# A diffusion-style block chain on one core: first modulation vectors by TensorE, and new places for the tiles

## The chip, the cores and the metric

The program runs on 1 core of a Trainium2 chip. The metric is the device time of one execution in microseconds. Everything is fp32 in memory; the big products use fp32r operands.

## What is computed

Two blocks in a row work on a sequence x of 512 tokens by 1024 features; the second also carries a context of 256 tokens. What matters here is how each norm is modulated: a condition vector c of 1024 numbers, through a SiLU, times a matrix w_ada, gives shift, scale and gate vectors of 1024 numbers each.

```python
def first_block(x, c, w_ada, b_ada, ...):
    c_act = jax.nn.silu(c)
    mod = c_act @ w_ada[l] + b_ada[l]                 # 6 vectors of 1024
    sh1, sc1, g1, sh2, sc2, g2 = jnp.split(mod, 6, axis=-1)
    h = _rmsnorm(x, norm_attn_g[l]) * (1.0 + sc1) + sh1
    proj = h @ w_in[l]                                # 3600 columns
    y = concat(dilated_attention(...), gated_deltanet(...)) @ w_out[l]
    x = x + g1 * y
    h = _rmsnorm(x, norm_ffn_g[l]) * (1.0 + sc2) + sh2
    x = x + g2 * ((silu(h @ w_gate[l]) * (h @ w_up[l])) @ w_down[l])
    return _rmsnorm(x, final_norm_g)

def second_block(x, c, ctx, c_ctx, ...):              # 2 layers
    # per layer: 9 vectors for the sequence and 9 for the context;
    # half step of a feed-forward, mixers (Fourier, attention, gating, pooling), half step
```

## The kernel before

**Products.** A big product x @ w is made by TensorE in three passes over fp32r halves: high(w) with high(x), high(w) with low(x), low(w) with high(x) (L2099, L2100, L2101 in this order; L2112 to L2114 where two blocks of weights go through the tiles in turn). A block of weights is 128 by 1024 numbers (8 tiles of 128 by 128); SyncE's queue loads it into one of 4 stage buffers (L1652), ScalarE rounds it to its high half (L1771), VectorE subtracts for the low half (L2544). The operand that streams is a tile of x with the 512 tokens of the sequence, or the 256 of the context, as columns: `hn_high`/`hn_low` after a norm, `hidden_high`/`hidden_low` inside a feed-forward, `mixed_high`/`mixed_low` after the mixers.

**Modulation.** `modulation` (16 calls in the opening, the others as background between the products) takes a block of w_ada as 128 partitions by 8 steps by 128 columns. The partitions are four quarters of 32, each for other columns; a partition holds 32 rows of the matrix in four parts; four DMAs, one for each quarter of the partitions, load a block. VectorE multiplies it by the condition and adds, 8 instructions per block (L2626 the first, L2629 the rest), and after four blocks TensorE sums over the partitions with two fp32 products (L2164), whose result gets the bias (L2634).

**Opening.** `first_block` starts with 16 such blocks: the vectors for scale and shift of the first norm. Between them it turns the tokens (L2205, four 128 by 128 transposes for each of 8 feature tiles), squares them (L1830) and sums the squares with fp32 products of one column (L2174), takes the root, and makes the rows of distances for the attention's bias (L2214, then a DMA out and back). `gains`, `modulated_norm` and the first products with w_in follow. Each engine walks the same program and runs its own part of it in order, with semaphores between the engines; a wait keeps everything behind it on its engine.

**Places.** `Memory` gives out the bytes of a partition in order. The permanent tiles come first (hidden state, stage, halves of the weights, the square buffers); the maps of the phases (`start_maps`, `first_maps`, `ffn_maps`, `mixer_maps`) then lie over each other from `phase_base` on. Before the change phase_base lies at 192 modulo 512:

```python
ROW, LANE = 512, 192
self.at += (LANE - self.at) % ROW     # before phase_base
self.at += (LANE - self.at) % 128     # before hn_first of the first block
```

As every tile in those maps is a multiple of 512 bytes long, except the padded convolution input (12 x 515 numbers), the streaming operands start at these places modulo 512: 448 for the first block's norm, 192 for its mixed tiles, for all tiles of the feed-forwards and for norm and mixed tiles of the mixers. The weights' halves start at 128.

Of the kernel before, what the change touches and what calls it, by code (L numbers as in the profile page):

```python
# [18 lines left out]
ALU = mybir.AluOpType  # L19
# [3 lines left out]
P = 128  # L23
# [22 lines left out]
QROWS = D // 32  # L46
ROW, LANE = 512, 192
COMPUTE = ("tensor_wrote", "scalar_wrote", "vector_wrote", "pool_wrote")
# [109 lines left out]
class Memory:  # L158


    def __init__(self, nc, ctx, inp, const, out):
# [22 lines left out]
        self.small_consts = sb("small_consts", [P, P])  # L184
        self.at += (LANE - self.at) % ROW
        self.phase_base = self.at
# [12 lines left out]
    def place(self, name, shape, dtype=F32):  # L199
        size = 4 * int(np.prod(shape[1:]))  # L200
        assert self.at + size <= SBUF_END, (name, self.at + size - SBUF_END)
        self.names += 1
        t = self.nc.alloc_sbuf_tensor_at(f"{name}_{self.names}", shape, dtype, offset=self.at)
        self.at += (size + 31) // 32 * 32
        return t

    def area(self, name, n):
# [8 lines left out]
    def start_maps(self):  # L216
# [30 lines left out]
        self.tokens_main = self.area("tokens", 4 * D).rearrange("p (a n) -> p a n", a=4)  # L247
        self.cond_rows = self.area("cond_rows", 3 * QROWS).rearrange("p (c n) -> p c n", c=3)
        self.table = self.area("table", SKEW)[0:N_BUCKETS + 1]
        self.relb = self.area("rel_bias", HEADS1)[0:N_BUCKETS + 1]  # L250
# [6 lines left out]
    def first_maps(self):  # L257
# [4 lines left out]
        self.G, self.EG, self.BT = (self.area("gate_rows", SEQ)[0:8] for _ in range(3))  # L262
        self.at += (LANE - self.at) % 128
        delta_base = self.at
# [20 lines left out]
        self.pick_pair = self.spread[0:8, 0:4, :]  # L285
        self.at = after_norms
        self.Y = self.halves("mixed", KT, SEQ)
        self.YD = self.tiled("delta_out", 4, SEQ)
# [4 lines left out]
    def ffn_maps(self):  # L293
        self.at = self.phase_base
        self.ffn_hn, self.hidden = {}, {}
        for name, T in (("ctx", CTX), ("main", SEQ)):
            self.ffn_hn[name] = self.halves("hn", KT, T)
            self.hidden[name] = self.halves("hidden", GROUPS[0][1], T)

    def mixer_maps(self):  # L300
# [5 lines left out]
        self.mixer = {"main": main, "ctx": side}  # L306
        for m, T in ((main, SEQ), (side, CTX)):
            m.T, m.nt, hn_at = T, T // P, self.at
            m.hn = self.halves("hn", KT, T)
            after, self.at = self.at, hn_at  # L310
            m.YS = self.halves("mixed", KT, T)
            m.YT = []
            for half in range(2):
                self.at = hn_at + 4 * (half * KT + 2) * T
                m.YT += [self.area("head_fourier", 2 * GW) for _ in range(T // GW)]
            self.at = after
# [81 lines left out]
class Walk:  # L398
# [82 lines left out]
    def load(self, n):  # L481
        w, k0, nk, c0, cols, split = self.board.plan[n]
        stage = self.stages.next()
        raw = stage.ap[:, 0:nk * cols]
        dst, at, moves = raw.rearrange("p (k n) -> p k n", k=nk), 0, []
        if isinstance(k0, tuple):
            rows = w.rearrange("(p r) n -> p r n", r=QROWS)[:, k0[0]:k0[0] + nk]
            moves = [(dst[32 * q:32 * q + 32], rows[:, :, c0 + q * P:c0 + (q + 1) * P]) for q in range(4)]
        for c, width in () if moves else (c0 if isinstance(c0, tuple) else ((c0, cols),)):
            moves.append((dst[:, :, at:at + width], w[k0:k0 + nk * P, c:c + width].rearrange("(k p) n -> p k n", p=P)))  # L490
            at += width
        self.load_block(n, stage, moves)
        return stage, raw
# [294 lines left out]
    def distance_bias(self):  # L788
        self.distance_tables()
        for o, n in ((0, 512), (512, SKEW - 512)):  # L790
# [816 lines left out]
    modulation_vector = clear = load_start = turn_vectors = condition = turn_tokens = distance_tables = idle  # L1607
    load_first = load_conditions = distance_rows = store_distances = skew_distances = token_square = token_pair = token_pair_sums = turn_context = gate_logs = gate_sums = gate_exps = turn_gates = load_bias = attention_scores = attention_turn = attention_values = idle
    attention_normalise = head_square = head_roots = head_spread = gains = clear_pads = gate_row = idle
# [9 lines left out]
class Sync(Walk):  # L1619


    def load_first(self):
        self.dma(self.misc(), ("eye",), self.mem.eye[:], self.mem.const["eye"])
        self.wait_ge("cleared")
        for n, (tile, dst, src) in enumerate(self.mem.rows):
# [3 lines left out]
    def load_start(self):  # L1629
        mem, i = self.mem, self.mem.inp  # L1630
        col = lambda ap: ap.rearrange("(n o) -> n o", o=1)
        self.dma(self.misc(), ("tokens", "main"), mem.tokens_main, i["x"][0].rearrange("(a p) n -> p a n", p=P))
        self.dma(self.misc(), ("small", 0), mem.dt_bias, col(i["dt_bias"][0]))
# [131 lines left out]
class Scalar(Walk):  # L1765
# [44 lines left out]
    def load_conditions(self):  # L1810
        i = self.mem.inp
        for n, c in enumerate((i["c"][0], i["c_2"][0], i["c_ctx_2"])):
            sem, rows = "cond_landed" if n == 0 else "conds_landed", c.rearrange("(p r) -> p r", r=QROWS)
# [3 lines left out]
            self.board.new["cond_rows", n] = sem, self.dma_counts[sem]  # L1817

    def condition(self, n, x, t):
        self.wait_ge("cond_rows", 2 if n else 0)  # L1820
        self.wait_free(t)
# [261 lines left out]
class Tensor(Walk):  # L2083
# [65 lines left out]
    def root_of_both(self, main, twin, names, banks):  # L2149
# [389 lines left out]
class Vector(Walk):  # L2539
# [64 lines left out]
    def scale_tile(self, name, part, k, rinv, ready):  # L2604
# [3 lines left out]
            .then_inc(*self.mark("scaled", name, k))  # L2608

    def modulation_sums(self, name, n, view, part, vectors, quarter):  # L2610

# [433 lines left out]
```

## Time and profile before

| what | us |
|---|---|
| median of 3 runs | 3629.4 (3621.26 to 3639.6) |
| profiled execution | 3635.35 |
| its span, first to last instruction | 3633.3 |

The profile is one execution. PE stands for TensorE's matmuls, PEld for its weight loads, DVE for VectorE, ACT for ScalarE, POOL for GpSimd, SP for SyncE; SPq and ACTq are DMA issues on these queues. A program's fp32 product stands in the records as two instructions (two loads, two matmuls); an fp32r product and a transpose as one. A matmul's listed duration runs past the start of the next one, so prices are read from start to start.

### The profile page before, as it was taken

Reading aid. Unit: us, or ns where it says so; the run is one execution under the profiler, and the core shown is the slowest. Engines: PE = TensorE matmul, PEld = TensorE weight load, DVE = VectorE, ACT = ScalarE, POOL = GpSimd, SP = SyncE. Lnnn points to the kernel's source line nnn. Section 1 sums busy time; section 2 is a strip of 40 time slices with the busy share of each in tenths; the row PEclk is TensorE's granted clock in tenths of the full one; section 3 lists DMA queues with packets and bytes.
Section 4 is the critical chain, followed back from the end, with each engine's and each line's share of the span. In section 5 each row is a group of like instructions: output and inputs, shape, how many; then the busy total and the mean of one; then the engine's idle time right before and its main releaser. Section 6 shows DMA issues by size and latency. Waiting matters only on the chain. (4 is left out here: it accounts for less than half of the span.)

```text
span 3633.3 us, 49233 instructions
## 1 busy us (share of the span) xinstructions
PE 3441.9 (95%) x19911; PEld 2821.2 (78%) x19911; DVE 2148.4 (59%) x4936; ACT 1031.6 (28%) x1604; POOL 131.9 (4%) x116
## 2 busy tenths in 40 slices
PE   5988899999999999899999999989999999999998
PEld 4655867887888888774688888878888886578887
DVE  6554656567667575764455667676766636543334
ACT  3354023222321212243432121222122124432222
POOL 0012010000000000100000000010000010000000
PEclk9998979999999999898999999989999999999999
DMA  8532024444234343330023434333343413023331
GB/s 176 148 96 64 4 74 125 118 132 115 85 91 116 99 115 94 99 85 18 24 62 99 113 93 111 101 106 87 107 107 102 109 49 111 12 76 95 97 99 64
DMA packets 646938, 333.94 MB, mean 92 GB/s; under 512 B 31659, under 2 KB 642935, under 8 KB 646456
## 3 DMA queue, kind: packets, MB, share of 16 engines
q1 hardware_dynamic: 645812, 330.63, 33.4%
q8 instruction: 156, 2.56, 0.3%
q14 instruction: 70, 0.57, 0.1%
q10 hardware_dynamic: 900, 0.18, 0.0%
HBM read 328.61 MB, written 2.77 MB: 91 GB/s over the span
## 5 line engine op out<-in xcount | busy, mean ns | idle before, releaser
L2099 PE MATMUL psum<-hn_high,high 128*128 128x512 f32 (+1 forms) x3136 | 1116.1, 356 | 9.7 <-DVE low L2544 9.7
L2101 PE MATMUL psum<-hn_high,low 128*128 128x512 f32 (+1 forms) x3136 | 1110.5, 354 | 0.0
L2100 PE MATMUL psum<-hn_low,high 128*128 128x512 f32 (+1 forms) x3136 | 1107.5, 353 | 0.0
L2629 DVE SCALAR_TENSOR_TENSOR partial<-stage,cond,partial 128x128 f32<-128x128 f32 x2592 | 701.9, 346 | 0.0
L2099 PEld LDWEIGHTS psum<-hn_high,high 128*128 128x128 f32 x3136 | 591.6, 189 | 120.5 <-issue 21.0
L2100 PEld LDWEIGHTS psum<-hn_low,high 128*128 128x128 f32 x3136 | 591.7, 189 | 86.5 <-issue 0.5
L2101 PEld LDWEIGHTS psum<-hn_high,low 128*128 128x128 f32 x3136 | 591.1, 188 | 82.8
L2544 DVE TENSOR_TENSOR low<-stage,high 128x1024 fp32r<-128x1024 f32 (+2 forms) x415 | 493.1, 1208 | 187.8 <-ACT high L1771 187.3
L1771 ACT ACTIVATE high<-stage 128x1024 fp32r<-128x1024 f32 (+2 forms) x415 | 415.2, 1025 | 504.0 <-DMA stage<-in_w_ffn 354.8
L2099 PE MATMUL psum<-hidden_high,high 128*128 128x512 f32 (+1 forms) x1408 | 495.8, 352 | 2.0 <-DVE hidden_low L2549 2.0
L2101 PE MATMUL psum<-hidden_high,low 128*128 128x512 f32 (+1 forms) x1408 | 496.4, 353 | 0.0
L2100 PE MATMUL psum<-hidden_low,high 128*128 128x512 f32 (+1 forms) x1408 | 495.4, 352 | 0.0
L2872 DVE TENSOR_TENSOR tmp<-tmp,psum 128x512 f32<-128x512 f32 (+1 forms) x176 | 103.5, 588 | 389.6 <-PE psum L2101 389.2
L1775 ACT ACTIVATE hidden_high<-tmp 128x512 fp32r<-128x512 f32 (+1 forms) x176 | 97.1, 552 | 791.8 <-DVE tmp L2872 791.8
L2099 PEld LDWEIGHTS psum<-hidden_high,high 128*128 128x128 f32 x1408 | 267.6, 190 | 40.6 <-DVE hidden_low L2549 2.4
L2100 PEld LDWEIGHTS psum<-hidden_low,high 128*128 128x128 f32 x1408 | 267.5, 190 | 38.3
L2101 PEld LDWEIGHTS psum<-hidden_high,low 128*128 128x128 f32 x1408 | 267.4, 190 | 35.3
L1992 ACT ACTIVATE tmp<-psum 128x512 f32<-128x512 f32 (+1 forms) x176 | 91.2, 518 | 359.7 <-PE psum L2101 346.2
L2869 DVE TENSOR_TENSOR tmp<-tmp,psum 128x512 f32<-128x512 f32 (+1 forms) x176 | 102.7, 584 | 112.0 <-ACT tmp L1992 112.0
L2549 DVE TENSOR_TENSOR hidden_low<-tmp,hidden_high 128x512 fp32r<-128x512 f32 (+1 forms) x176 | 104.3, 593 | 108.8 <-ACT hidden_high L1775 108.8
L1731 POOL TENSOR_TENSOR mean_main<-mean_main,tmp 128x512 f32<-128x512 f32 x42 | 54.5, 1297 | 2726.5 <-ACT tmp L1793 2726.5
L2763 DVE SCALAR_TENSOR_TENSOR h_main<-psum,small,h_main 128x512 f32<-128x512 f32 x96 | 71.6, 746 | 75.2 <-PE psum L2101 75.0
(316 smaller groups left out, 2948.3 us busy)
## 6 DMA issues: line engine op xcount, KB each, us to landing
stage<-in_w_ffn SPq DMA_DIRECT2D x240, 512.0 KB, 4.2
stage<-in_w_ada SPq DMA_DIRECT2D x768, 128.0 KB, 2.8
stage<-in_w_in SPq DMA_DIRECT2D x48, 512.0 KB, 4.5
stage<-in_w_out SPq DMA_DIRECT2D x24, 512.0 KB, 4.1
stage<-in_w_ffn SPq DMA_DIRECT2D x32, 384.0 KB, 3.8
stage<-in_w_gate SPq DMA_DIRECT2D x22, 512.0 KB, 3.9
stage<-in_w_up SPq DMA_DIRECT2D x22, 512.0 KB, 5.1
stage<-in_w_down SPq DMA_DIRECT2D x16, 512.0 KB, 4.0
```

The source lines that it names most:

```text
L1771: self.e.activation(high, raw, ACT.Copy).then_inc(*self.mark("high", n))
L1775: self.e.activation(high, x, ACT.Copy).then_inc(*self.mark("high_half", key))
L1992: self.e.activation(s, ps_a, ACT.Sigmoid).then_inc(*self.mark("gate_sigmoid", key))
L2099: self.e.matmul(out, high[:, i], xh, start=first and n == 0, stop=False)
L2100: self.e.matmul(out, high[:, i], xl, start=False, stop=False)
L2101: done = self.e.matmul(out, low[:, i], xh, start=False, stop=last and n == nk - 1)
L2544: self.e.tensor_tensor(low, raw, high.bitcast(F32), ALU.subtract).then_inc(*self.mark("split", n))
L2549: self.e.tensor_tensor(low, x, high.bitcast(F32), ALU.subtract).then_inc(*self.mark(*key))
L2629: self.e.scalar_tensor_tensor(acc, view[:, k, :], by, acc, ALU.mult, ALU.add).then_inc(*inc)
L2763: self.e.scalar_tensor_tensor(h, ps, gate, h, ALU.mult, ALU.add).then_inc(*self.mark("residual", name, part.name, f))
L2869: self.e.tensor_tensor(s, s, ps_a, ALU.mult).then_inc(*self.mark("gated", key))
L2872: self.e.tensor_tensor(s, s, ps_b, ALU.mult).then_inc(*self.mark("gated_up", key))
```

## The change

The opening's 16 blocks are taken by TensorE: block j holds rows p*8 + k of w_ada (p the partition, k = j modulo 8) with 1024 columns, of the scale for j under 8 and of the shift after; it is loaded by one DMA in rows of 4 KB, and 8 fp32 products with the column k of the condition add to 8 columns of one PSUM bank. One VectorE instruction then adds the bias to all 16 columns. The condition of the first block gets a load and a SiLU of its own; the other conditions, the late vectors, the distance table and the tokens are loaded or taken at other points. The streaming operands of the sequence start at 384 modulo 512 and those of the context at 64.

```diff
-ROW, LANE = 512, 192
+ROW, MAIN_LANE, CTX_LANE = 512, 384, 64
...
-        self.at += (LANE - self.at) % ROW
+        self.lane(CTX_LANE)
         self.phase_base = self.at
...
+    def lane(self, at):
+        self.at += (at - self.at) % ROW
...
         self.G, self.EG, self.BT = (self.area("gate_rows", SEQ)[0:8] for _ in range(3))
-        self.at += (LANE - self.at) % 128
+        self.lane(MAIN_LANE)
         delta_base = self.at
...
         self.at = after_norms
+        self.lane(MAIN_LANE)
         self.Y = self.halves("mixed", KT, SEQ)
...
-        for name, T in (("ctx", CTX), ("main", SEQ)):
+        for name, T, lane in (("ctx", CTX, CTX_LANE), ("main", SEQ, MAIN_LANE)):
+            self.lane(lane)
...
-        for m, T in ((main, SEQ), (side, CTX)):
+        for m, T, lane in ((main, SEQ, MAIN_LANE), (side, CTX, CTX_LANE)):
+            self.lane(lane)
...
-        if isinstance(k0, tuple):
+        if isinstance(k0, tuple) and cols > P:
+            moves = [(dst, w.rearrange("(p r) n -> p r n", r=KT)[:, k0[0]:k0[0] + nk, c0:c0 + cols])]
+        elif isinstance(k0, tuple):
...
         self.load_first()
-        self.take_condition(0)
-        self.take_vectors(0, 1)
+        self.open_condition()
         self.load_start()
+        self.distance_tables()
...
-        squares = []
+        squares, opening = [], self.mix.next()
         for j in range(2 * KT):
-            one(j)
+            k, half = j % KT, 1 - j // KT
+            n, stage, view = self.weights(i["w_ada"][0], (k,), 1, half * D, D, split=False)
+            self.open_products(j, n, view[:, 0, :], half, k, opening)
+            stage.free = [("opened", j)]
             if j == 3:
+                self.take_vectors(0, 1)
+            if j == 13:
+                for c in range(3):
+                    self.take_condition(c)
                 self.take_vectors(1, 3)
-                self.take_condition(1)
-                self.take_condition(2)
...
-            if k == KT + 1:
+            if k == KT:
                 self.distance_bias()
...
-        self.finish_modulation()
+        self.open_vectors(opening, mod[:, 0:2 * KT, 0], bias[:, 0:2 * KT])
+        opening.free = self.mod_ready = [("opened_vectors",)]
...
     def load_first(self):
         self.dma(self.misc(), ("eye",), self.mem.eye[:], self.mem.const["eye"])
+        self.dma(self.misc(), ("tokens", "main"), self.mem.tokens_main, ...)
...
     def load_conditions(self):
+        self.dma_counts["cond_landed"] = 16
+        self.e.dma_start(self.mem.cond_first[:, 0, :], i["c"][0].rearrange("(p r) -> p r", r=KT)) \
+            .then_inc(self.sems["cond_landed"], 16)
...
+    def open_products(self, j, n, w, half, k, bank):
+        self.wait_ge("landed", n)
+        self.wait_ge("cond_first_silu")
+        if j == 0:
+            self.wait_free(bank)
+        for b in range(KT):
+            at = half * KT + b
+            done = self.e.matmul(bank.ap[:, at:at + 1], w[:, b * P:(b + 1) * P], self.mem.cond_first[:, 1, k:k + 1],
+                                 start=j == b == 0, stop=k == KT - 1, skip_group_check=True)
+        done.then_inc(*self.mark("opened", j))
...
+    def open_vectors(self, bank, mod, bias):
+        self.wait_ge("opened", 2 * KT - 1)
+        self.wait_ge("vec", 0)
+        self.e.tensor_tensor(mod, bank.ap[:, 0:2 * KT], bias, ALU.add).then_inc(*self.mark("opened_vectors"))
```

## Rows read from the trace of the kernel before

**Rows 1.** the page's head and part 1 (busy time of each engine).
```profile
span 3633.3 us, 49233 instructions
...
PE 3441.9 (95%) x19911; PEld 2821.2 (78%) x19911; DVE 2148.4 (59%) x4936; ACT 1031.6 (28%) x1604; POOL 131.9 (4%) x116
```

**Rows 2.** busy time by stretches: PE, PEld, DVE, ACT, POOL, clock, DMA share, GB/s.
```profile
20.00:40.00 20.00, 12.17 (x55) 11.47 (x56) 20.00 (x78) 6.37 (x13) 0.00 (x0) 1.00 1.17 225
```

**Rows 3.** groups of instructions by line, first 60 us.
```profile
L2629 DVE SCALAR_TENSOR_TENSOR partial<-stage,cond,partial 128x128 f32<-128x128 f32 x120 | 32.4, 343 | 0.0
...
L2174 PEld LDWEIGHTS psum<-ones,tmp 128*128 128x128 f32 x32 | 7.1, 328 | 6.7 <-DVE tmp L2654 6.7
L2205 PEld LDWEIGHTS psum<-eye,tokens 128*128 128x128 f32 x32 | 7.0, 243 | 0.0
...
L2214 PE MATMUL psum<-table,rel_bias 33*8 33x512 f32 (+1 forms) x4 | 2.3, 725 | 3.2 <-DMA rel_bias<-in_rel_bias 3.2
...
L2145 PEld LDWEIGHTS psum<-eye,small 128*128 128x128 f32 x8 | 1.8, 327 | 3.0 <-DVE small L2591 3.0
```

**Rows 4.** timeline, opening and its end: start us, us, engine line op.
```profile
4.62 1.95 ACTq L1816 DMA_DIRECT2D cond_rows<-in_c_ctx  x4
...
8.16 0.19 DVE L2664 TENSOR_TENSOR cond<-cond_rows,tmp 128x32 f32<-128x32 f32 x1 [6.27 <-ACT tmp L1822]
...
58.33 1.01 PE L2164 MATMUL psum<-quarter,partial 128*128 128x4 f32 x4
...
64.06 0.62 PE L2112 MATMUL psum<-hn_high,high 128*40 128x512 f32 x1 [4.72 <-DVE hn_low L2602]
```

**Rows 5.** timeline of PE before the second block.
```profile
943.33 1.05 PE L2133 MATMUL psum<-ones,tmp 128*128 128x1 f32 x8 [0.73 <-ACT tmp L1793]
944.24 1.03 PE L2129 MATMUL psum<-ones,root 128*128 128x1 f32 x8
```

**Rows 6.** busy time and granted clock by stretches, end of a feed-forward.
```profile
2993.20:2996.60 3.40, 3.40 (x34) 3.40 (x32) 0.80 (x3) 1.93 (x4) 0.00 (x0) 0.99 0.02 5
2996.60:3000.00 3.40, 2.85 (x14) 2.77 (x13) 2.22 (x7) 1.13 (x2) 0.98 (x1) 0.50 0.35 101
```

**Rows 7.** DMA issues in the first 60 us.
```profile
stage<-in_w_ada SPq DMA_DIRECT2D x68, 128.0 KB, 3.7
```

**Rows 8.** groups of PE by line and shape, whole span.
```profile
L2099 PE MATMUL psum<-hn_high,high 128*128 128x512 f32 x2024 | 803.6, 397 | 9.7 <-DVE low L2544 9.7
...
L2099 PE MATMUL psum<-hidden_high,high 128*128 128x512 f32 x880 | 348.5, 396 | 2.0 <-DVE hidden_low L2549 2.0
...
L2099 PE MATMUL psum<-hn_high,high 128*128 128x256 f32 x1080 | 301.7, 279 | 0.0
...
L2099 PE MATMUL psum<-hidden_high,high 128*128 128x256 f32 x528 | 147.3, 279 | 0.0
```

**Rows 9.** timeline of PE, first block's products, tiles at 448 modulo 512.
```profile
118.02 0.39 PE L2099 MATMUL psum<-hn_high,high 128*128 128x512 f32 x1
...
125.57 0.39 PE L2099 MATMUL psum<-hn_high,high 128*128 128x512 f32 x1
```

**Rows 10.** timeline of PE, second block, layer 1, sequence and context products.
```profile
2599.82 0.39 PE L2101 MATMUL psum<-hidden_high,low 128*128 128x512 f32 x1
...
2602.11 0.28 PE L2099 MATMUL psum<-hidden_high,high 128*128 128x256 f32 x1
...
2604.71 0.28 PE L2101 MATMUL psum<-hidden_high,low 128*128 128x256 f32 x1
```

**Rows 11.** timeline of PE, first feed-forward, tiles at 192.
```profile
571.72 0.40 PE L2099 MATMUL psum<-hn_high,high 128*128 128x512 f32 x1
...
577.32 0.40 PE L2099 MATMUL psum<-hn_high,high 128*128 128x512 f32 x1
```

**Rows 12.** timeline of PE, second block, layer 0, context products.
```profile
1101.54 0.28 PE L2099 MATMUL psum<-hidden_high,high 128*128 128x256 f32 x1
...
1104.25 0.28 PE L2101 MATMUL psum<-hidden_high,low 128*128 128x256 f32 x1
```

More of the change, by code:

```diff
@@ L248, in start_maps @@
         self.cond_rows = self.area("cond_rows", 3 * QROWS).rearrange("p (c n) -> p c n", c=3)
+        self.cond_first = self.area("cond_first", 2 * KT).rearrange("p (c n) -> p c n", c=2)
         self.table = self.area("table", SKEW)[0:N_BUCKETS + 1]
@@ L788, in distance_bias @@
     def distance_bias(self):
-        self.distance_tables()
         for o, n in ((0, 512), (512, SKEW - 512)):
@@ L1607 @@
     modulation_vector = clear = load_start = turn_vectors = condition = turn_tokens = distance_tables = idle
-    load_first = load_conditions = distance_rows = store_distances = skew_distances = token_square = token_pair = token_pair_sums = turn_context = gate_logs = gate_sums = gate_exps = turn_gates = load_bias = attention_scores = attention_turn = attention_values = idle
+    open_condition = open_products = open_vectors = load_first = load_conditions = distance_rows = store_distances = skew_distances = token_square = token_pair = token_pair_sums = turn_context = gate_logs = gate_sums = gate_exps = turn_gates = load_bias = attention_scores = attention_turn = attention_values = idle
     attention_normalise = head_square = head_roots = head_spread = gains = clear_pads = gate_row = idle
@@ L1623, in load_first @@
         self.dma(self.misc(), ("eye",), self.mem.eye[:], self.mem.const["eye"])
+        self.dma(self.misc(), ("tokens", "main"), self.mem.tokens_main, self.mem.inp["x"][0].rearrange("(a p) n -> p a n", p=P))
         self.wait_ge("cleared")
@@ L1631, in load_start @@
         col = lambda ap: ap.rearrange("(n o) -> n o", o=1)
-        self.dma(self.misc(), ("tokens", "main"), mem.tokens_main, i["x"][0].rearrange("(a p) n -> p a n", p=P))
         self.dma(self.misc(), ("small", 0), mem.dt_bias, col(i["dt_bias"][0]))
@@ L1811, in load_conditions @@
         i = self.mem.inp
+        self.dma_counts["cond_landed"] = 16
+        self.e.dma_start(self.mem.cond_first[:, 0, :], i["c"][0].rearrange("(p r) -> p r", r=KT)) \
+            .then_inc(self.sems["cond_landed"], 16)
+        self.board.new["cond_first",] = "cond_landed", 16
         for n, c in enumerate((i["c"][0], i["c_2"][0], i["c_ctx_2"])):
-            sem, rows = "cond_landed" if n == 0 else "conds_landed", c.rearrange("(p r) -> p r", r=QROWS)
+            sem, rows = "conds_landed", c.rearrange("(p r) -> p r", r=QROWS)
             for q in range(4):
@@ L1817, in load_conditions, with open_condition @@
             self.board.new["cond_rows", n] = sem, self.dma_counts[sem]
+    def open_condition(self):
+        self.wait_ge("cond_first")
+        self.e.activation(self.mem.cond_first[:, 1, :], self.mem.cond_first[:, 0, :], ACT.Sigmoid) \
+            .then_inc(*self.mark("cond_first_sigmoid"))
     def condition(self, n, x, t):
-        self.wait_ge("cond_rows", 2 if n else 0)
+        self.wait_ge("cond_rows", 2)
         self.wait_free(t)
@@ L2608, in scale_tile, with open_condition @@
             .then_inc(*self.mark("scaled", name, k))
+    def open_condition(self):
+        raw, act = self.mem.cond_first[:, 0, :], self.mem.cond_first[:, 1, :]
+        self.wait_ge("cond_first_sigmoid")
+        self.e.tensor_tensor(act, raw, act, ALU.mult).then_inc(*self.mark("cond_first_silu"))
+    def open_vectors(self, bank, mod, bias):
+        self.wait_ge("opened", 2 * KT - 1)
+        self.wait_ge("vec", 0)
+        self.e.tensor_tensor(mod, bank.ap[:, 0:2 * KT], bias, ALU.add).then_inc(*self.mark("opened_vectors"))
     def modulation_sums(self, name, n, view, part, vectors, quarter):
```

## The prediction

> **What bounds the kernel now.** I read the page's busy times first [rows 1]: TensorE (PE) is busy for 3441.9 of 3633.3 us. So a change is worth what it does to the time from one big product to the next, or to the stretches in which PE doesn't run big products yet. The second kind is the opening. There the stretches of time [rows 2] show VectorE (DVE) busy for all of 20 to 40 us and PE for 12.2 us of it, and the groups by line [rows 3] name the work: 120 steps of L2629, 32.4 us, which multiply a block of w_ada by the condition and add. The timeline [rows 4] gives its ends: the condition is ready on DVE at 8.16 + 0.19 = 8.35 us, the sum over partitions of the last shift vectors (L2164) starts at 58.33 and ends at 59.34, and the first product of hidden state and w_in starts 4.7 us later, at 64.06. From 64 us on PE is nearly full, so what the opening gains or loses in that 59.34 reaches the end whole.
>
> **Part one, the opening.** Removed: 16 blocks with 8 steps of DVE each, and four small sums on PE. Put in their place: 16 blocks with 8 fp32 products each, 128 rows by 128 columns of weights against one column of the condition. The trace has this very form: L2174, which sums squares. A program's fp32 product is two instructions in the records (16 such products of L2174 are x32), and 32 weight loads took 7.1 us, 0.222 us each [rows 3]. That is the lower of its two clock levels (1.2 GHz); the clock column's 1.00 in the opening [rows 2] doesn't fit that price, and I go by the price. So 128 products are 256 loads: 256 x 0.222 = 56.8 us, 3.55 us a block.
>
> Does PE stay at that level? Before the second block the same form follows big products at the upper level (2.4 GHz): L2133 starts at 943.33 and L2129, eight instructions later, at 944.24, 0.114 us each [rows 5]. At that price the 256 would take 29.2 us. But after a stretch that is almost all such small products, in which PE was busy for 3.40 of 3.40 us, the granted clock is 0.50 in the next stretch [rows 6]: full occupation with them did not hold the upper level. I take the low level for the whole opening, which starts at it and holds only such products, transposes of 128 columns and one pair of wider ones. The Trainium skill says the opposite for this stream ("TensorE: Matmul & The Clock Gate", section "Why this matters for your kernels": a TensorE that is kept busy without pause gets the full clock, and loses it by idling). By that rule the opening would cost 29.2 instead of 56.8 us; the trace disagrees with it where it shows 3.40 busy us and then 0.50.
>
> The rest of PE's opening stays and now stands in the same queue: transposes of the tokens 7.0, sums of squares 7.1, distance rows 2.3, the root spread over the tokens 1.8 [rows 3], and three transposes of vectors, which I price by L2205's 0.22 us as 0.7: 18.9 us. It can start when the condition is there. ScalarE (ACT) now issues one DMA more ahead of it, 1.95 / 4 = 0.49 us, so DVE ends the condition at 8.35 + 0.49 = 8.84 and PE begins at about 9.0 [rows 4]. Sum: 9.0 + 56.8 + 18.9 = 84.7 us, against 59.34: **+25 us**. The stride between loads in L2174 includes short waits at the ends of four products; without them I would expect nearer 0.21, so the sum can be 2 us less, and waits between unlike jobs can add as much. I take **+24**.
>
> What is hidden: a block of 512 KB is now one DMA of 4 KB rows. A 128 KB piece lands 3.7 us after its issue [rows 7], and at the 225 GB/s of [rows 2] a block needs 2.3 us, less than the 3.55 us that PE spends on it, so from four buffers on DMA isn't late; at PE's warm price (1.8 us) it would be. Larger pieces might go faster; nothing waits for it. The tokens are issued earlier and the distance table too; both were ready early enough already and are wanted later now. SP's queue holds 16 fewer times three issues, which no one then waits for. The conditions of the second block and the late vectors move behind block 13: ACT and DVE do them in 3 x 0.2 us while PE has a block of 3.5 us, and their readers are the later modulations. The root (ACT, with its table load, and DVE) has block 14 as cover; without it, it would cost some 2.5 us. The tail from the last sum to the first big product, 4.7 us, stays: both kernels then add the bias, form the gain, split w_in and norm a tile. DVE is free for 30 us that nobody uses, since what it does next hangs on the same vectors.
>
> **Part two, the places of the tiles.** By the allocator's arithmetic the fp32r operands that stream through PE start at 448 modulo 512 in the first block's norm and at 192 everywhere else; they move to 384 (512 columns wide) and 64 (256 wide). Weights stay at 128. The number of such products: 2024 + 880 per line with 512 columns and 1080 + 528 with 256, times three lines, 8712 and 4824, and a tenth more in smaller groups [rows 8]. What does the place do? At 448, 33 starts take 7.55 us, 0.2288 us each [rows 9]; at 192, ten take 2.29 us, 0.229 [rows 10]. Two places, one price. But at one and the same place there are two prices: in the first feed-forward 24 starts take 5.60 us, 0.2333 each [rows 11], and the context's products take 0.1178 (23 in 2.71 us) in layer 0 [rows 12] and 0.1130 (23 in 2.60) in layer 1 [rows 10]. So some state other than the address sets a price, and the address might choose it. The bounds: all 256-wide products at 0.1130 instead of half of them at 0.1178 (by my reading of the timeline the slower price holds from about 981 to 1502, 1561 to 1963 and 2400 to 2525 us) is 5300 / 2 x 0.0048 = 13 us of gain; all 512-wide ones at 0.2333 is 9600 x 0.0043 = 41 us of loss; and as gain for those I know only twice the 256-wide fast price, 0.226, 9600 x 0.003 = 29 us. I take nothing, since the only two places that the trace compares agree, and keep -42 and +41 as bounds. DVE's and ACT's tiles move too, but PE, not they, is what the big stages wait for.
>
> **Sum.** The profiled execution took 3635.35 us (span 3633.3), the median of the runs is 3629.4. On either I add 24; on the median: **3653 us**.
>
> **Rivals.**
> (a) The tiles' places make products faster, and this decides the sign: from 24 / 9600 = 2.5 ns a 512-wide product on, the change is not slower. Speaks for it: two prices at one place exist, so a collision of reads is there to be avoided; against it: 448 and 192 cost the same to 0.1%. With both gains (29 + 13) the time is 3629 + 24 - 42 = 3611; if more than 0.226 is to be had, it is faster still.
> (b) Only the context's products gain: 3653 - 13 = 3640.
> (c) The places make the 512-wide ones go at 0.2333: 3653 + 41 = 3694.
> (d) The opening runs at the upper level after all: 9.0 + 29.2 and about half of 18.9 is 47.7, and DMA, 10 MB at 225 GB/s, 46 us, agrees. Then 59.3 - 47.7 = 12 us of gain: 3618. Against it stands [rows 6]. The Trainium skill's rule on a busy TensorE (cited above) would bring it about.
> (e) That part two does nothing is my likeliest case itself.
>
> **Chances.** Likeliest (cold opening, places neutral) 0.43, own range 3645 to 3664. (a) 0.24, (b) 0.14, (c) 0.11, (d) 0.08. The measurement tells about 0.5% from no change, 18 us: faster is below 3611, slower above 3648. Faster: most of (a), 0.19, and 0.03 of (d): 0.22. Same: (b), 0.05 each of (a) and (d), and the low end of the likeliest, 0.09: 0.33. Slower: 0.34 and (c): 0.45. The range leaves out the deep end of (a) and most of (c): 3595 to 3675.
>
> **What would show it.** In the new trace: weight loads of the opening 0.21 to 0.22 us apart, in groups of 16; PE busy from 9 us on with hardly a gap; the last of them near 83 us and the first product of w_in near 88. If they are 0.11 apart, (d) holds. The places: starts in a run of 512-wide products 0.229 apart, or not, and 256-wide at 0.113 or 0.118, read in the same stages as here. I would be wrong by the first if another wait sits in PE's new queue (a bank, the late rows), and by the second if 384 or 64 differ from the two places that I could read.

## The result, and the profile after

| | us |
|---|---|
| kernel before, median of 11 runs | 3632.95 (3621.26 to 3647.12) |
| changed kernel, median of 11 runs | 3652.8 (3645.27 to 3655.91) |
| ratio after / before | 1.0044 [1.0025, 1.0062] |
| spans of the profiled executions | 3633.3 before, 3653.0 after |

The changed kernel is slower by 0.25 to 0.62%, and the medians of this comparison lie 19.9 us apart. The forecast of 3653 us was met to 0.2 us. Part of that agreement is luck: it stood on a first median of 3629.4, which came out as 3632.95 over more runs, so the predicted step was 24 us and the measured one 20.

The page's head and busy times, to be held against [rows 1]:

```profile
span 3653.0 us, 49525 instructions
...
PE 3486.5 (95%) x20151; PEld 2883.5 (79%) x20151; DVE 2115.6 (58%) x4806; ACT 1032.3 (28%) x1605; POOL 131.9 (4%) x116
```

VectorE (DVE) lost 32.8 us of work and TensorE (PE) gained 44.6; 128 steps of the condition (120 of L2629, 8 of L2626) went from the engine with room to the engine that bounds. The stretches of the opening (columns as in [rows 2]):

```profile
20.00:40.00 20.00, 20.00 (x98) 20.00 (x97) 0.98 (x2) 3.41 (x7) 0.00 (x0) 1.00 0.46 134
40.00:60.00 20.00, 20.00 (x98) 20.00 (x97) 1.38 (x2) 4.29 (x9) 0.00 (x0) 1.00 0.36 105
60.00:80.00 20.00, 20.00 (x89) 18.12 (x88) 1.89 (x7) 5.10 (x11) 0.00 (x0) 1.00 0.45 119
```

PE is now full where DVE was full, and DVE does 1 to 2 us of 20. The DMA share falls from 1.17 to about 0.4: the new form needs no more than 134 GB/s. The group of the new weight loads, from those up to the first big product:

```profile
L2188 PEld LDWEIGHTS psum<-cond_first,stage 128*128 128x128 f32 x256 | 56.1, 333 | 9.5 <-issue 9.5
```

And the timeline of its end, beside [rows 4] (L2188 is a block's products with the condition, L2653 adds the bias, L2135 is the first big product):

```profile
72.32 3.53 PEld L2188 LDWEIGHTS psum<-cond_first,stage 128*128 128x128 f32 x16
...
75.80 2.05 PE L2168 MATMUL psum<-eye,small 128*128 128x128 f32 x8
...
77.65 3.41 PE L2188 MATMUL psum<-cond_first,stage 128*128 128x1 f32 x16
81.10 0.17 DVE L2653 TENSOR_TENSOR mod<-psum,vec 128x16 f32<-128x16 f32 x1 [7.92 <-PE psum L2188]
...
85.79 0.62 PE L2135 MATMUL psum<-hn_high,high 128*40 128x512 f32 x1 [4.73 <-DVE hn_low L2637]
```

The last product with the condition ends at 77.65 + 3.41 = 81.06 us, 21.7 us after the 59.34 of before, and the tail to the first big product is 4.7 us as before: 85.79 against 64.06. So the whole difference at the end, 19.7 us in span, is already there before any big product has run.

The places, read in the stages of [rows 11], [rows 10] and [rows 12]. First feed-forward, 512 columns:

```profile
596.77 0.39 PE L2135 MATMUL psum<-hn_high,high 128*128 128x512 f32 x1
...
602.21 0.39 PE L2122 MATMUL psum<-hn_high,high 128*128 128x512 f32 x1
```

24 starts take 5.44 us, 0.2267 each, where [rows 11] had 0.2333. Second block, layer 1, context, 256 columns:

```profile
2621.75 0.28 PE L2122 MATMUL psum<-hidden_high,high 128*128 128x256 f32 x1
...
2624.22 0.28 PE L2122 MATMUL psum<-hidden_high,high 128*128 128x256 f32 x1
```

21 starts take 2.47 us, 0.1176 each, where [rows 10] had 0.1130. One price fell and the other rose.

Which level the clock had in the opening can be read too. The trace of the changed kernel holds no record of the granted clock before 91.38 us; the first one says 1.00, and around it the starts of the 512-wide products go from 0.43 us apart (those at 90.05 and 90.48) to 0.23 (91.59 and 91.82). In the kernel before the first record is at 67.93 us, with the same step in the starts. So both openings, and the first few big products, ran at the lower level (1.2 GHz), and the 1.00 that the tables print there stands for no record.

### The profile page after: what moved, and what is told of

Same layout as the page of the kernel before. It is cut to its first block and busy times, and to the rows that moved or that the text cites. A ratio compares the mean times of both kernels' runs of the same rounds, so it can differ in the third digit from the quotient of the medians.

```text
span 3653.0 us, 49525 instructions
## 1 busy us (share of the span) xinstructions
PE 3486.5 (95%) x20151; PEld 2883.5 (79%) x20151; DVE 2115.6 (58%) x4806; ACT 1032.3 (28%) x1605; POOL 131.9 (4%) x116
## 5 line engine op out<-in xcount | busy, mean ns | idle before, releaser
L2122 PEld LDWEIGHTS psum<-hn_high,high 128*128 128x128 f32 x3136 | 591.7, 189 | 115.8 <-issue 22.5
L2674 DVE SCALAR_TENSOR_TENSOR partial<-stage,cond,partial 128x128 f32<-128x128 f32 x2472 | 669.4, 346 | 0.0
```

Source lines behind the costliest of these rows:

```text
L2122: self.e.matmul(out, high[:, i], xh, start=first and n == 0, stop=False)
L2674: self.e.scalar_tensor_tensor(acc, view[:, k, :], by, acc, ALU.mult, ALU.add).then_inc(*inc)
```

## A count of every product, and of where the time went

To see the prices over the whole span, take from each trace all groups of three products (high by high, low by high, high by low) that follow one another without anything between, from the start of one group to the start of the next. All in all there are 3216 groups of the wide kind (512 columns) and 1736 of the narrow (256); those that other work interrupts, that are the last of their row or that ran at the lower clock are left out. In the kernel before the starts fall on few values, 687 and 700 ns for the wide groups, 340 and 353 for the narrow; the ranges of the columns are in ns. Distance is the place of the streaming tile less that of the weights, modulo 256.

| kernel | distance, sequence / context | wide 675-682 | 683-688 | 689-697 | 698-710 | mean | narrow 336-342 | 343-355 | 356-365 | mean |
|---|---|---|---|---|---|---|---|---|---|---|
| before | 64 / 64 | 0 | 2681 | 29 | 110 | 687.2 | 807 | 739 | 8 | 346.5 |
| changed | 0 / 192 | 2641 | 27 | 145 | 6 | 680.8 | 63 | 1490 | 2 | 352.8 |

What this is worth can be summed without choosing groups, since both kernels run the same 14976 products in the same order: take the time from each product's start to the next one's, and subtract. Where it is steady in both (under 245 ns for a wide product, under 125 for a narrow one), the 9333 wide ones come to -19.3 us and the 5099 narrow ones to +10.6. The rest, in which PE waits, runs other work or has the lower clock, comes to +6.7, and with +21.7 up to the first product this makes the +19.7 of the last one. The starts of single products show where the rest lies (product 100 is the one with 100 before it):

| product | before | changed | difference | places only (below) | with it |
|---|---|---|---|---|---|
| first | 64.1 | 85.8 | +21.7 | 63.6 | -0.5 |
| 100 | 89.0 | 111.5 | +22.5 | 89.1 | +0.1 |
| 150 | 107.1 | 131.8 | +24.7 | 109.7 | +2.6 |
| 650 | 322.3 | 345.8 | +23.5 | 325.6 | +3.3 |
| 700 | 499.6 | 526.0 | +26.4 | 507.1 | +7.5 |
| 7000 | 1947.9 | 1965.0 | +17.1 | 1949.3 | +1.4 |
| last | 3609.2 | 3628.9 | +19.7 | 3613.2 | +4.0 |

Two steps against the gain stand out, between products 100 and 150, and in the deltanet stage between 650 and 700, where PE walks through thousands of small products. The stretches of time, same work in each, of before and then of the changed kernel:

```profile
89.00:107.10 18.10, 15.02 (x68) 11.93 (x67) 11.68 (x31) 5.52 (x7) 0.00 (x0) 0.86 0.48 117
322.30:499.60 177.30, 154.24 (x3108) 124.86 (x3107) 97.47 (x161) 28.61 (x51) 9.96 (x12) 0.79 0.05 10
```

```profile
111.50:131.80 20.30, 14.96 (x68) 11.96 (x67) 11.71 (x31) 5.49 (x7) 0.00 (x0) 0.85 0.44 105
345.80:526.00 180.20, 157.76 (x3107) 125.97 (x3106) 97.39 (x161) 28.66 (x51) 9.97 (x12) 0.77 0.04 10
```

In the deltanet stage the instructions, DVE's and ACT's busy times are the same, PE's waits are too (23.1 us not busy against 22.4), and only PE's busy time grew, by 3.5 us. By the trace's records of the granted clock the lower level held for 83.1 us of this stretch against 73.3 before. This stage has short gaps all over; the same work got the lower level for 9.8 us more, which at half speed can cost up to 4.9.

In the stretch of products 100 to 150 it is not the clock. The lower level held for 6.3 us against 5.0 and PE's busy time is the same, but PE waits for 2.3 us more, all of it at one place, before the products of L2226 (L2261 in the changed kernel). First before, then changed:

```profile
99.54 1.06 ACT L1771 ACTIVATE high<-stage 128x1024 fp32r<-128x1024 f32 x1 [5.13 <-DMA stage<-in_w_in]
102.59 0.35 PE L2226 MATMUL psum<-eye,gate_rows 8*128 8x8 f32 x2 [2.53 <-DVE gate_work L2724]
```

```profile
124.21 1.06 ACT L1785 ACTIVATE high<-stage 128x1024 fp32r<-128x1024 f32 x1 [7.33 <-DMA stage<-in_w_in]
127.26 0.35 PE L2261 MATMUL psum<-eye,gate_rows 8*128 8x8 f32 x2 [4.74 <-DVE gate_work L2769]
```

A block of w_in is issued equally early in both, 5.9 us after product 100 starts, but lands 4.61 us after its issue before and 6.77 after it in the changed kernel; ACT's rounding, DVE's subtraction and then the step that PE waits for stand behind it. Why this transfer took longer is open.

## Experiments

In the expectations "distance" is as in the table above. Letters A to C, E, G and H are explained where they are used. Of the places, two theories come back several times: each product's price comes from the distance of its own streaming tile to the weights (D); or the context's price hangs on the state in which the sequence's products leave TensorE, whatever its own place (F).

**The two parts alone.** e1_places_only is the kernel before with the new places (and self.lane before each group of tiles, as in the change):

```diff
-ROW, LANE = 512, 192
+ROW, MAIN_LANE, CTX_LANE = 512, 384, 64
-        self.at += (LANE - self.at) % ROW
+        self.lane(CTX_LANE)
...
-        self.at += (LANE - self.at) % 128
+        self.lane(MAIN_LANE)
```

> The kernel before with the new places alone (sequence at 384, context at 64), VectorE's opening kept. Theory A, places set the prices: sequence products 0.2267 us apart instead of 0.229 (3216 groups of three x 7 ns = -22 us), context products at 0.1177 almost everywhere instead of half of them (+11 us), so about -11 us, 3622 against 3633; first big product at 64 us. Rival B, the later start of the products sets the prices and the places do nothing: prices as before, time as before within 4 us, and the new prices turn up in the run with the new opening alone.

Measured: 3629.37 us (3624.79 to 3639.42, 12 runs) against 3634.24 for the kernel before, ratio 0.9991 [0.9975, 1.0006]. The prices moved as theory A says (wide groups 680.8 ns in the mean, 2640 of 2828 at 680; narrow 352.9), so rival B is out; but the step of 4.9 us is not clear of nothing, where A wanted 11. The profiled execution, with a span of 3637.3, was the slowest of the twelve. In it the steady wide products give 19.1 us and the steady narrow ones cost 10.9, and the rest costs 12.8: 2.5 us at products 100 to 150, 4.2 in the deltanet stage, and some 6 elsewhere that nothing here explains. The block of w_in is late again (7.11 us from issue to landing), and the lower clock held for 6.8 us of the first stretch below and 83.3 of the second (columns as before):

```profile
89.10:109.70 20.60, 14.94 (x68) 11.93 (x67) 11.68 (x31) 5.50 (x7) 0.00 (x0) 0.83 0.45 103
325.60:507.10 181.50, 159.54 (x3108) 126.48 (x3107) 97.79 (x161) 28.66 (x51) 9.96 (x12) 0.77 0.04 10
```

e2_opening_only is the changed kernel with all tiles where they were (the reverse of the diff above).

> The changed kernel with the old places, so TensorE's opening alone. Theory A: first big product at 85.8 us, 21.7 us later than before, later prices as before (0.229; context half at 0.113, half at 0.118), time +22 us, 3655. Rival B: prices 0.2267 and 0.1177 here too, time about +17. If the 9 us of loss that the prices leave open in the changed kernel belong to the opening (colder or later neighbours), the time here is +31, 3664.

Measured: 3661.56 us (3657.44 to 3672.11, 6 runs), ratio 1.0078 [1.0053, 1.0102], span 3659.0. The first big product starts at 86.1, 22.0 us late, and the last one 25.7 us late. Of the wide groups 2161 are at 687 and 637 at 700; of the narrow ones 981 at 340 and 563 at 353. 518 wide groups in one piece, from 3268 us to the end, are 13 ns dearer than in the kernel before, 6.7 of the 6.9 us by which all steady wide products are slower; 174 more narrow groups are at the low price (-2.6 us over all narrow ones). The expectation had a branch for a time near 3664, colder or later neighbours; the time came near it, but in this trace what lies beyond the opening's 22 us is this piece and not lower clock or waits (the rest comes to -0.6 us). In it the groups look like this:

```profile
3399.98 0.40 PE L2119 MATMUL psum<-hn_high,high 128*128 128x512 f32 x1
...
3407.68 0.40 PE L2119 MATMUL psum<-hn_high,high 128*128 128x512 f32 x1
```

11 groups take 7.70 us, 700 ns each, at the places where the kernel before pays 687. So at distance 64 the price isn't fixed; it changes within one execution at unchanged places. Whether the piece at 700 comes with the new opening or was chance in this one execution is not shown. The opening alone is enough for the slowdown: it costs 27 us here, 22 of them before the first big product. The changed kernel, with the new places too, is 9 us faster than this one by the medians, but the two were not measured side by side and their intervals overlap.

**Which place does it.** e3_ctx_192 is e1 with the context left at 192 (CTX_LANE = 192).

> VectorE's opening, sequence at 384, context and the phases' base at 192. Theory A with a price for each width by its own place: sequence products 0.2267 (-22 us), context as before, half at 0.113: 3611, some 11 us below the run with both new places. Rival C, the context's price hangs on the neighbouring sequence products and not on its own place: context at 0.1177 here too, time as in the run with both new places.

Measured: 3636.24 us (3629.36 to 3641.54, 12 runs), ratio 1.0001 [0.9984, 1.0017], span 3635.2. Of the wide groups 2273 are at 680 and 558 above it, up to 698 (mean 682.3); of the narrow ones 1398 at 353, 143 at 356 or 357, and 12 at 340. The prices are those of rival C, and the 11 us that theory A wanted did not come. In the stage of [rows 10]:

```profile
2604.27 0.28 PE L2105 MATMUL psum<-hidden_high,high 128*128 128x256 f32 x1
...
2606.75 0.28 PE L2105 MATMUL psum<-hidden_high,high 128*128 128x256 f32 x1
```

7 groups in 2.48 us, 354 ns each, where the same context tile at the same place cost 340 in [rows 10]. The context's tile stayed where it was and lost its low price because the sequence's tiles moved, so its own distance alone doesn't set its price.

e4_weights_448 moves the weights instead of the tiles, so that sequence and context both have distance 0:

```diff
+        self.at += 320
         self.high = [sb(...)
...
+        self.at += 192
         self.tmp = sb("tmp", ...)
```

> The kernel before with the six halves of the weights moved from 128 to 448 modulo 512, the streaming tiles left at 192 (448 in the first block's norm). Theory D, what counts is the distance between the streaming tile and the weights: 192 - 448 is 256 modulo 512 like the changed kernel's 384 - 128, so sequence products go at 0.2267 outside the first norm, about -18 us. Rival E, the streaming tile's own place counts: prices as before, time as before within 5 us.

Measured: 3642.01 us (3637.28 to 3647.88, 10 runs), ratio 1.002 [1.0003, 1.0036], span 3641.5. Of the wide groups 2429 are at 680 and 384 at 689 or more (mean 681.8). First feed-forward:

```profile
575.61 0.39 PE L2101 MATMUL psum<-hn_high,high 128*128 128x512 f32 x1
...
581.73 0.39 PE L2101 MATMUL psum<-hn_high,high 128*128 128x512 f32 x1
```

9 groups in 6.12 us: 680 ns with the tile at 192, where [rows 11] has 700 with the same tile. What counts for the wide products is where tile and weights lie to one another, not the tile's own place. In the first block's norm the tile has the same place as the weights modulo 512 (448), and there the groups take 680 ns too, so a distance of 0 and one of 256 cost the same. The whole isn't faster, since the narrow products got a third price, 360 ns a group, that the kernel before doesn't have (1389 of 1552 clean groups lie at 356 or more, mean 359.2):

```profile
2579.43 0.28 PE L2101 MATMUL psum<-hn_high,high 128*128 128x256 f32 x1
...
2584.47 0.28 PE L2101 MATMUL psum<-hn_high,high 128*128 128x256 f32 x1
```

14 groups in 5.04 us. The steady wide products give 16.5 us and the narrow ones cost 21.7.

Four kernels, each measured in a single execution beside one of the kernel before at 3638.05, fill in the other distances; differences of a few us in their times say nothing, the prices in their traces do: l1_d128_d0 (MAIN_LANE, CTX_LANE = 256, 384), l2_d192_d128 (320, 256), l3_main192_ctx64 (192, 64) and l4_main384_ctx256 (384, 256), all with the opening of before.

> VectorE's opening; sequence at 256, context at 384 modulo 512; distance from the weights (128) modulo 256: sequence 128, context 0. Theory D (distance modulo 256 sets the price): the sequence's price at 128 is unknown, the context's at 0 too; if 0 is good for both widths the context goes at 0.113. Theory F (the context's price is set by the phase that the sequence's products leave): context at one fixed price that goes with the sequence's.

> VectorE's opening; sequence at 320 (distance 192), context at 256 (distance 128). Theory D: by the two distances so far, 0 is 0.2267 and 64 is 0.229 or 0.2333 for the sequence; 192 should be like 64 if it is a matter of alignment to 128, otherwise a new price. Theory F: the context has 0.113 and 0.118 in turn wherever the sequence has 0.229.

> VectorE's opening; sequence at 192 as before, context alone at 64. Theory D: context at 0.1177 everywhere, as in the changed kernel. Theory F: context at 0.113 and 0.118 in turn, as before.

> VectorE's opening; sequence at 384 as in the changed kernel, context at 256 (distance 128). Theory D: sequence 0.2267, the context's price new. Theory F: context at 0.1177 as with 64 and 192, since the sequence is at 0.2267.

| kernel | distance | us | wide 675-682 | 683-688 | 689-697 | 698-710 | mean | narrow 336-342 | 343-355 | 356-365 | mean |
|---|---|---|---|---|---|---|---|---|---|---|---|
| l1_d128_d0 | 128 / 0 | 3685.79 | 0 | 2 | 1573 | 1262 | 697.4 | 0 | 190 | 1357 | 358.8 |
| l2_d192_d128 | 192 / 128 | 3687.57 | 0 | 3 | 694 | 2132 | 699.8 | 0 | 921 | 633 | 355.8 |
| l3_main192_ctx64 | 64 / 192 | 3641.75 | 0 | 2637 | 38 | 153 | 687.6 | 67 | 1492 | 1 | 352.4 |
| l4_main384_ctx256 | 0 / 128 | 3640.52 | 2312 | 26 | 376 | 116 | 682.5 | 0 | 189 | 1367 | 359.4 |

The products of l2_d192_d128 in the first feed-forward:

```profile
595.70 0.40 PE L2105 MATMUL psum<-hn_high,high 128*128 128x512 f32 x1
...
601.29 0.40 PE L2105 MATMUL psum<-hn_high,high 128*128 128x512 f32 x1
```

8 groups in 5.59 us, 699 ns. Distance 0 gives 680, 64 gives 687 and at times 700, 192 mostly 697 to 703, and 128 values from 690 to 706. For the narrow ones neither theory holds as put. l3 leaves the sequence as it was and moves only the context, and the low price is gone but for 67 groups, which F doesn't allow; e3 moves only the sequence, and it is gone too, which D doesn't allow. But D is right in part: with the sequence at distance 0 the context costs 353 at distances 64 and 192 (e3, e1), and 360 at 0 and 128 (e4, l4). The low price of 340 held for whole stages only with both at distance 64 (before and e2), and there for half to two thirds of the groups; 47 to 67 groups have it in the changed kernel, e1, l3 and o1 as well. What chooses it stays open.

Subtracted product by product from the kernel before, as above, in us up to the start of the last big product:

| kernel | first product | wide, steady | narrow, steady | rest | last product |
|---|---|---|---|---|---|
| changed | +21.7 | -19.3 | +10.6 | +6.7 | +19.7 |
| e1_places_only | -0.5 | -19.1 | +10.9 | +12.8 | +4.0 |
| e2_opening_only | +22.0 | +6.9 | -2.6 | -0.6 | +25.7 |
| e3_ctx_192 | -0.1 | -15.1 | +11.9 | +5.3 | +2.0 |
| e4_weights_448 | +0.1 | -16.5 | +21.7 | +2.8 | +8.2 |
| l1_d128_d0 | -0.4 | +30.9 | +20.9 | -1.0 | +50.4 |
| l2_d192_d128 | -0.7 | +37.9 | +15.5 | -0.8 | +51.9 |
| l3_main192_ctx64 | -0.7 | +1.0 | +10.2 | -4.0 | +6.5 |
| l4_main384_ctx256 | -0.6 | -14.6 | +21.9 | -1.2 | +5.6 |
| o1_condition_still (below) | -3.0 | -19.3 | +10.8 | +1.0 | -10.5 |

The two middle columns belong to the places; the rest differs by several us between kernels with the same places (e1 and o1).

**The opening, in another form.** The last question is whether the opening had to be slow. o1_condition_still keeps all of the changed kernel but turns the operands of the 128 products round: a column of the condition is what TensorE loads, and the block of w_ada streams as two times 512 columns. The sums then lie in one partition as four lines of 512; ScalarE and DVE copy them out, and 16 small products with a one turn them into columns.

```diff
-        for b in range(KT):
-            done = self.e.matmul(bank.ap[:, at:at + 1], w[:, b * P:(b + 1) * P],
-                                 self.mem.cond_first[:, 1, k:k + 1], ...)
+        for c in range(2):
+            done = self.e.matmul(line.ap[0:1, :], self.mem.cond_first[:, 1, k:k + 1],
+                                 w[:, 512 * c:512 * (c + 1)], start=k == 0, stop=k == KT - 1)
...
+        for b in range(KT):
+            done = self.e.matmul(bank.ap[:, at:at + 1], self.mem.open_line[:, at * P:(at + 1) * P],
+                                 self.mem.ones[0:1, 0:1], start=True, stop=True)
```

> The changed kernel with the operands of the opening's products exchanged: the condition's column is the weight (one column to load), the block's 1024 columns stream as two products of 512, 4 instructions a block instead of 16; 16 small products then turn the line into columns. Theory A, the opening is bound by 256 loads of 128 columns at the low clock and wide products get the high one: a block 1.7 us instead of 3.5, 16 blocks 27 us, the other jobs at half price 10, lines into columns 4: last one near 52 us, first big product near 57, time some 28 us under the changed kernel, 3625. Rival G, the low clock stays in the opening whatever streams: 0.85 us a product instruction, 3.4 us a block, no gain, 3653 or more. Rival H, the blocks' DMAs bind as soon as PE is faster: first big product at 9 + 16 x 2.3 + 5 = 50 to 60 us and PE idle between the blocks.

Measured: 3625.23 us (3620.36 to 3627.13, 12 runs) against 3633.29 for the kernel before, ratio 0.9971 [0.9957, 0.9985], span 3622.8. Its timeline, two loads of the first blocks on either side of 13.5 us, one block further on, and the end:

```profile
12.73 0.13 PEld L2200 LDWEIGHTS psum<-stage,cond_first 128*1 128x1 f32 x1 [0.72 <-issue]
13.53 0.09 PEld L2200 LDWEIGHTS psum<-stage,cond_first 128*1 128x1 f32 x1 [0.67 <-issue]
13.96 0.08 PEld L2200 LDWEIGHTS psum<-stage,cond_first 128*1 128x1 f32 x1 [0.34 <-issue]
...
24.30 1.88 PE L2200 MATMUL psum<-stage,cond_first 128*1 128x512 f32 x4
...
50.64 1.16 PE L2181 MATMUL psum<-eye,small 128*128 128x128 f32 x8
...
61.05 0.62 PE L2148 MATMUL psum<-hn_high,high 128*40 128x512 f32 x1 [4.74 <-DVE hn_low L2660]
```

The first big product starts at 61.05, 24.7 us before that of the changed kernel and 3.0 before that of the kernel before. Where does that come from? Up to 13.5 us the instructions start 0.85 us apart, from there on 0.43, and 13.46 us is where the trace has its first record of the granted clock, with 1.00. So this opening, whose first product starts at 9.37 us, went to the upper level (2.4 GHz) at 13.46, and stayed there until 57.8 us, where the record says 0.50. The other jobs show it too: the eight products of the root take 1.16 us here (L2181) and 2.05 in the changed kernel (L2168). A block is 4 instructions: 4 x 0.853 = 3.41 us at the lower level, to the hundredth what the changed kernel spends on its 16 loads there (16 x 0.213), and 1.7 at the upper. And 16 loads at the upper level would take 16 x 0.114 = 1.8 us, an estimate from [rows 5]. So at one level the two orders of the operands cost the same, and what turning them round gained is the level: here the clock rose within the opening, in the changed kernel only once the big products ran. Theory A holds, with 3625 us as expected, though its first big product was to come near 57 and not at 61. Rival G is out from 13.5 us on.

Rival H is out too. DMA is closer to the path, its share is 0.79 over the first 60 us at 227 GB/s, but PE waits for a block for only 0.8 us in all (groups of the opening):

```profile
L2200 PE MATMUL psum<-stage,cond_first 128*1 128x512 f32 x64 | 31.6, 626 | 10.2 <-DVE cond_first L2671 9.4 <-DMA stage<-in_w_ada 0.8
```

Further on its prices are those of e1 (wide 680.8 ns in the mean, narrow 352.9). The same two stretches once more:

```profile
85.90:102.20 16.30, 12.93 (x67) 10.28 (x66) 10.38 (x27) 5.43 (x7) 0.00 (x0) 1.00 0.55 130
318.00:496.20 178.20, 156.65 (x3108) 125.75 (x3107) 97.58 (x161) 28.66 (x51) 9.96 (x12) 0.79 0.04 10
```

With the same big products and the same places, products 100 to 150 take 16.3 us here and 20.6 in e1. 2.3 us of this is the late block of w_in (4.84 us from issue to landing here, 7.11 in e1), and PE's busy time is 2.0 us less, with no lower level in the stretch against 6.8 us of it. The deltanet stage takes 178.2 against 181.5, with 76.6 us at the lower level against 83.3. So these few us do not belong to the tiles' places; they go with the landing of one block and with the time at the lower clock. This version is faster than the kernel before by 0.15 to 0.43%, and by some 27 us than the changed one, though not measured side by side with it. Its lead over the kernel before is not all the opening's: of the 10.5 us in the traces the opening gives 3.0, and most of the rest comes with the places.

## Why the prediction was right

**The mechanism of the opening** held: it stands in PE's queue whole, at the low level. The rows are there: 256 loads from 9.04 us on, PE busy for 20.00 of 20.00 us in three stretches, and the clock's first record at 91.38 us. What was sized too high is the price of a load: 0.222 was read from L2174 with the waits at its ends in it, and a block of 16 takes 3.41 us, 0.213 each. 256 x 0.213 = 54.6; the other work and all transitions took 81.06 - 9.04 - 54.6 = 17.4 where 18.9 stood. The sum of 84.7 came out as 81.06, the step of +24 as +21.7. The prediction had said that nearer 0.21 was to be expected and then gave most of that back for transitions that didn't come.

**Full occupation and the clock.** The Trainium skill ("TensorE: Matmul & The Clock Gate", section "Why this matters for your kernels") says that a TensorE kept busy gets the full clock. The rows say otherwise for this stream: PE is without a gap for the 60 us shown and a load still costs 0.213 us, nearly twice the 0.114 of [rows 5]. The granted clock is printed as 1.00 in these stretches, in this kernel as in [rows 2], where the trace has no record yet; the prediction went by the price against that column, and rightly. By the Trainium skill's rule the 256 loads would have taken 256 x 0.114 = 29 us instead of 54.6. In o1_condition_still, whose PE was busy for all of 20 to 40 us as well, the upper level did come.

**What was called hidden** was: the blocks land 3.6 us after their issue (3.7 predicted from pieces), DVE is nearly idle, the root's 0.20 and 0.18 us on ACT and DVE lie under block 14, and its table load and the conditions of the second block under block 13. The tail stayed at 4.7.

**The places** were the step that failed in its content and held in its sum. I took them as neutral because the only two places to be compared cost the same. They do, and now one sees why: 448 and 192 both lie 64 modulo 256 from the weights, so the trace held one distance twice, and the comparison could not speak about a third. In truth the wide products gained 19.3 us, against a bound of 29, and the narrow ones lost 10.6 in place of staying or gaining 13. Rival (a) was right that places make products faster, by 2.1 ns each over the steady ones where it needed 2.5. Rival (b) had the sign of the context wrong. Rival (c) was the real danger: distance 192 costs 38 us on the wide products and 128 costs 31, near the 41 that it names, the narrow ones add 16 to 21 (l2, l1), and the change could as well have landed there. Rival (d) is out for this kernel; its mechanism, the upper level in the opening, is what o1 shows with the operands turned round.

**The total.** In us, from the traces: +21.7 opening, -19.3 wide products, +10.6 narrow ones, and +6.7 of the rest, of which 2.9 lie in the deltanet stage, 2.2 at the late block behind the opening and 1.6 elsewhere. This makes the 19.7 at the last product. So the forecast of 3653 has its main term right by argument, and its second term, zero, right by luck: three effects of 19, 11 and 7 us that it didn't foresee met at -2. The share of chance in it is of the order of 10 us, and the range of 3595 to 3675 was the honest statement. Of the three outcomes the ratio of 1.0044 (1.0055 by the medians alone) lies right at the bound of 0.5%, between "same" (0.33) and "slower" (0.45).

## What to carry to other kernels

Before moving work from a free engine to the bound one, ask at which clock level the bound engine will run it, and read the level from the prices, not from the clock column before its first record. Here a matrix against one vector cost TensorE 3.41 us a block at the lower level in either order of the operands; with the vector's column as weights and the matrix streaming the clock rose at 13.5 us and a block then cost 1.7; with the same places this turned +20 us into -8. If two operands in memory seem to have no effect of their places, check that the places differ in the quantity that matters, here the distance between tile and weights modulo 256. When counting prices, look at every value that occurs before sorting them into classes: of the narrow groups' three, 353 and 360 ns lie only 2% apart. And when the phases of a long kernel shift, expect a few us of either sign from a transfer that lands late or from stages with many short gaps; subtracting two traces product by product tells this from a real gain.

## What the runs showed of the hardware

- fp32r products of 512 columns cost by the distance from weights to streaming tile, start to start: 226.7 ns at distance 0 (also where it is 256 modulo 512), 229 at 64 and at times 233.3, 232 to 234 at 192, 230 to 235 at 128. At 64 both prices occur at one place, in long pieces of one execution.
- Those of 256 columns cost 113.3, 117.7 or 120 ns. 120 came with the context at distance 0 or 128 (e4, l1, l4, in part l2), 117.7 with it at 64 or 192. 113.3 held for whole stages only when the sequence's and the context's tiles both lay at distance 64, and not even then throughout. Which state chooses there wasn't found.
- An fp32 product instruction with 512 streaming columns starts 0.85 us before the next at the lower clock level and 0.43 at the upper (o1, on either side of 13.5 us); a load of 128 columns with one streaming column 0.213 (the changed kernel) and 0.114 ([rows 5]).
- The records of the granted clock begin with the first change: at 91.38 us in the changed kernel, 67.93 before, 13.46 in o1. Until then the tables print 1.00, and the prices are those of the lower level.
- The changed kernel's runs lie closer together, 3645.3 to 3655.9, than those of the kernel before, 3621.3 to 3647.1; those of o1 closer still, 3620.4 to 3627.1. Why is open: e1 has o1's places and spreads from 3624.8 to 3639.4.
